# 512-column bfloat16 products on TensorE, and an earlier masked product on VectorE, in two attention-like stages of a two-block network

## The reference, cut to what matters

```python
def one_block(args):                      # differential attention, 8 heads, blocks of 128 queries
    qblk, start = args
    s = jnp.einsum('bqhcd,bkhcd->bhcqk', qblk, k).astype(jnp.float32) * scale
    s = jnp.where(mask, s, -jnp.inf)
    p = jax.nn.softmax(s, axis=-1)
    attn = p[:, :, 0] - lam * p[:, :, 1]
    return jnp.einsum('bhqk,bkhe->bqhe', attn.astype(v.dtype), v)
...
# state-space mixer: 16 heads in 4 groups
cb = jnp.einsum("bclgn,bcsgn->bcgls", cm, bm)
y_diag = jnp.einsum("bcgls,bgecls,bcsgep->bclgep", cb, decay_in, x_dt)
states = jnp.einsum("bclgn,bgecl,bclgep->bcgepn", bm, decay_states, x_dt)
y_off = jnp.einsum("bclgn,bcgepn,bgecl->bclgep", cm, prev, jnp.exp(a_cum))
```

## Time and profile before

| | us |
|---|---|
| three runs shown | 3040.71, 3015.47, 3042.67; median 3040.71 |
| profiled execution, its own time | 3019.05 |
| its span | 3017.3 |
| TensorE busy in it | 2626.9 (87%) |
| VectorE busy | 1455.2 (48%) |
| ScalarE busy | 957.2 (32%) |
| mean granted clock of TensorE | 0.865 |

### The profile page before, as it was taken

One profiled execution on the slowest core, in us unless ns is written; L12 is line 12 of the kernel. 1 busy time (PEld: TensorE's weight loads), 2 busy tenths in 40 slices (PEclk: granted clock), 3 DMA queues, 4 the chain that ended last, 5 costly groups with the idle time before them and its releaser, 6 DMA issues.

```text
span 3017.3 us, 39461 instructions
## 1 busy us (share of the span) xinstructions
PE 2626.9 (87%) x16258; PEld 1729.5 (57%) x16258; DVE 1455.2 (48%) x2253; ACT 957.2 (32%) x1535; POOL 73.4 (2%) x60
## 2 busy tenths in 40 slices
PE   6979999999989886899998997757785989899997
PEld 5768878888878653544445445544443456444443
DVE  4773435552255355365324453454445343477742
ACT  3321223322232443332222332114443234343321
POOL 0610000000000000000000000000000000000000
PEclk9975578999979876799998995658897999999998
DMA  3100001232312200022321310000001133023221
GB/s 140 71 1 29 29 29 56 85 112 84 112 39 83 84 1 1 28 87 109 112 84 56 112 72 28 1 15 1 30 1 56 56 112 112 29 84 112 76 95 67
DMA packets 27731, 188.08 MB, mean 62 GB/s; under 512 B 3072, under 2 KB 3584, under 8 KB 6048
## 3 DMA queue, kind: packets, MB, share of 16 engines
q1 hardware_dynamic: 27072, 183.77, 16.6%
q10 hardware_dynamic: 480, 1.79, 0.2%
HBM read 183.45 MB, written 2.10 MB: 61 GB/s over the span
## 4 chain that ended last, share of the span: by engine, by line
PE 78%; DVE 13%; ACT 6%; issue 2%; DMA 1%; DVEq 0%; ACTq 0%; POOL 0%; SPq 0%; POOLq 0%
PE ps L428 37%; PE ps L425 20%; PE ps L538 3%; PE ps L1044 1%; DVE wsp L409 1%; ACT wsp L398 1%; PE ps L586 1%; PE ps L1390 1%; DVE wk L2486 1%; PE ps L1032 1%; PE ps L881 1%; PE ps L1412 1%; DMA raw_w<-slabs 1%; PE ps L556 1%; PE ps L948 1%
## 5 line engine op out<-in xcount | busy, mean ns | idle before, releaser
L428 PE MATMUL ps<-hn,wsp 128*128 128x512 f16 x3120 | 689.6, 385 | 28.9 <-DVEq L226 10.3
L428 PEld LDWEIGHTS ps<-hn,wsp 128*128 128x128 f16 x3120 | 308.2, 99 | 409.4 <-issue 30.4
L409 DVE SCALAR_TENSOR_TENSOR wsp<-raw_w,wsp 128x2048 f16<-128x2048 f32 (+1 forms) x176 | 389.7, 2214 | 316.3 <-ACT wsp L398 305.8
L428 PE MATMUL ps<-big,wsp 128*128 128x512 f16 (+2 forms) x2304 | 465.8, 364 | 5.0 <-DVE wk L2111 2.8
L425 PE MATMUL ps<-hn,wsp 128*128 128x264 f16 x3552 | 413.6, 280 | 13.3 <-DVE hn L378 7.8
L425 PEld LDWEIGHTS ps<-hn,wsp 128*128 128x128 f16 x3552 | 351.8, 99 | 74.1 <-issue 14.6
L398 ACT ACTIVATE wsp<-raw_w 128x2048 f16<-128x2048 f32 (+1 forms) x176 | 324.7, 1845 | 167.5 <-PE ps L425 66.4
L428 PEld LDWEIGHTS ps<-big,wsp 128*128 128x128 f16 (+1 forms) x2304 | 230.6, 100 | 233.8 <-issue 6.1
L425 PE MATMUL ps<-big,wsp 128*128 128x264 f16 x1920 | 218.9, 277 | 0.1
L425 PEld LDWEIGHTS ps<-big,wsp 128*128 128x128 f16 x1920 | 188.3, 98 | 30.0 <-ACT hn L415 0.3
L415 ACT ACTIVATE wk<-ps 128x512 f32<-128x512 f32 (+2 forms) x116 | 69.0, 595 | 346.9 <-PE ps L428 345.6
(11 more groups left out here) (353 smaller groups left out, 2744.6 us busy)
## 6 DMA issues: line engine op xcount, KB each, us to landing
raw_w<-slabs SPq DMA_DIRECT2D x166, 1024.0 KB, 5.2
raw_w<-slabs SPq DMA_DIRECT2D x8, 384.0 KB, 5.0
h<-xin SPq DMA_DIRECT2D x1, 2112.0 KB, 8.6
out<-hn SPq DMA_DIRECT2D x8, 256.0 KB, 2.8
big<-memx ACTq DMA_DIRECT2D x1, 1024.0 KB, 5.3
cst<-consts SPq DMA_DIRECT2D x1, 995.5 KB, 9.7
sml<-small SPq DMA_DIRECT2D x1, 768.0 KB, 12.1
wk<-ropes ACTq DMA_DIRECT2D x1, 528.0 KB, 3.7
```

What stands on the lines that cost most here:

```text
L409: L.fin(L.eng.scalar_tensor_tensor(wsp[:, n % NW, 1, lo:hi], raw_w[:, q % 2, 0:hi - lo], WSCALE, wsp[:, n % NW, 0, lo:hi], ALU.mult, ALU.s ...
L428: return L.eng.matmul(ps[:rows, b, 0:T], lhsT, rhs, start=start, stop=stop)
```

## The change

There are three edits. A new helper, `keep_warm(L, b, k)`, issues k matmuls on TensorE, each with the 128x128 bfloat16 identity `eye16` as weights and the first 512 bfloat16 values of the constant `ssd_mask` as the moving operand, into PSUM bank b. Nothing reads the result, and a later matmul with `start=True` overwrites the bank. It has four of them in each of the 16 units of the state-space part, between the wait for `mx` and the wait for `ysum`, and four in the 31 turns of the attention's loop that have a next unit, between its values and the transposes of the next one. And on VectorE the masked product of group g+1 now comes ahead of the sums of group g, and that of group 0 right after the chunk's `xw`.

```diff
+        def keep_warm(L, b, k):
+
+            for _ in range(k):
+                L.eng.matmul(ps[:, b, :], eye16, C("ssd_mask").bitcast(BF16)[:, 0:512], start=True, stop=True)
...
                     pe.wait_ge(sem("mx"), n + 1)
+                    keep_warm(L, r, 4)
                     pe.wait_ge(sem("ysum"), n) if n else None
...
                 l1_values(n)
                 if n + 1 < 32:
+                    keep_warm(L, 6, 4)
                     l1_turn_pe(n + 1)
...
+            def mixed(n):
+
+                L.take("dm")
+                L.fin(tt(Mx[:, n % 2, :, :], Dm[:, n % 2, :, :],
+                         ps[:, 2 + n % 2, 0:P].unsqueeze(1).to_broadcast([P, 4, P]), ALU.mult), "mx")
+
             for c in range(SSD_NC):
...
                 L.fin(tt(xw, xdt, dlast[:, c, :].unsqueeze(2).to_broadcast([P, 16, 64]), ALU.mult), "xw")
+                mixed(4 * c)
                 for g in range(4):
                     n = 4 * c + g
-                    L.take("dm")
-                    L.fin(tt(Mx[:, n % 2, :, :], Dm[:, n % 2, :, :],
-                             ps[:, 2 + n % 2, 0:P].unsqueeze(1).to_broadcast([P, 4, P]), ALU.mult), "mx")
+                    if g < 3:
+                        mixed(n + 1)
                     L.take("py")
```

## The result

Changed kernel: median 3007.8 us of 13 runs (2988.5 to 3010.4). Kernel before: median 3038.5 of 13 runs (3015.5 to 3044.2). The ratio is 0.9908, 95% interval 0.9887 to 0.9929: 28 us faster, or 22 to 34 by the interval (the two medians alone lie 30.7 us apart). The forecast on the median was 16 us less and a time of 3025; the time lies in the range given, but the gain is nearly twice the forecast one. At 0.9% by the ratio (0.7 to 1.1% by its interval) it stands at the very line of 1% at which the chances were divided, and it is clear of noise.

The account below looks back on a forecast made before the run. TensorE, busy 87% of the span, was taken to bound the kernel, with both stages partly at the low clock. Attention −9 and state-space −7 gave −16 us, from a median of 3041 to 3025 us, range 2994 to 3046.

Parts of the forecast that it names:

- What a group costs: Four added products on TensorE cost 0.85 us at the high clock or 1.7 us at the low one.
- the 18 us of the bound: Both stages: if weight loads lay between the products, 0.4 us more per group, 18 us for 47 groups.
- Attention, the clock and the place of the groups: Attention loop: clock stays high, groups of queries 0 and 1 hide in the output-copy wait; −9 us.
- The short units: Attention, queries 2 and 3: TensorE's work summed to 4.05 us each, against 4.50 and 4.71.
- The starting point: Profiled execution of 3019 us as base, less 16; median of 3041 lies 22 us above it, unexplained by the trace.
- State-space part: Clock gains of −5, −2 and −2, group costs of +4.5, VectorE's order −3: together −7 us.
- −5 for chunk 0: State-space chunk 0: three units at the high clock save 7.5 us; one unit lost before the clock rises leaves −5.
- a clock over 0.85 until the chunk's end: State-space part: granted clock expected if the forecast was right.
- The wait of about 1.1 us at group 3: State-space group 3: TensorE's expected wait for line 2050 behind the added group, if the forecast was right.
- VectorE's order: State-space part: masked product leaves the path, 0.73 us off group 3's wait, −3 us over 4 chunks.
- The rule about busy work: Skill's rule that sustained busy work releases the throttle; if true, the sum would be some 8 us worse in chunk 0.
- more than forecast: Rival: short attention units fall to 3.6 (16 us), all four chunks run high (12 us): −28, 3013; chance 0.10.

Follow-up runs that it names:

- e3: Kernel before with only VectorE's new order and no added products: 3031.7 us, ratio 1.0009 to the kernel before.
- e7: Changed kernel with four more products ahead of each of the 16 steps of the first block's recurrent mixer: 2969.5 us, ratio 0.9781 to the kernel before.
- e8: Changed kernel with the attention's products only in the turns of queries 0 and 1: attention 132.5 us, ratio 0.9848 to the kernel before.
- e9: Kernel before with four products per state-space unit, in bank 4 and ahead of the wait for `mx`, VectorE's old order: state-space part 111.6 us.
- e13: Changed kernel with the state-space products moved to bank 4 and ahead of the wait for `mx`, VectorE's new order: state-space part 115.0 us.
- e14: Changed kernel plus products in the recurrent mixer and at chunk ends, state-space products ahead of the wait, new order: 2962.2 us, ratio 0.9745 to the kernel before.
- e15: Changed kernel plus products in the recurrent mixer and at chunk ends, state-space products ahead of the wait, but old order: 2964.9 us, ratio 0.9751 to the kernel before.
- e4: Changed kernel with added products of 16 rows instead of 128, same 512 columns: 3075.1 us, ratio 1.0165 to the kernel before.

## Why the prediction was right or wrong

**What a group costs: right.** 0.87 us at the high clock (0.85), loads hidden: with 188 products in two stages the 18 us of the bound did not appear.

**Attention, the clock and the place of the groups: right.** The clock is 0.96 (0.95 or more was asked), the steps 4.18 and 4.78 (4.19 and 4.77), the whole 132.3 us (about 132). The whole agrees in part by luck. The short units are shorter than summed, 3.78 and 3.77 instead of 4.05: the sum divided the duration of a group by its count, but in the rows each starts before the one ahead of it has ended: after the six values the next group starts 0.87 us on (1061.98 to 1062.85), not 1.0, and after the four transposes 0.44 us on (1064.14 to 1064.58), not 0.7. A few steps with a fall of the clock make up for it, which the sum did not have; the changed kernel's second profile has 134.8.

**The starting point: this is the step that failed.** Between the two profiles the stages shrank by 14.7 us, near the 16 forecast. What failed is that the kernel before was taken to be as its one profile shows it, and that the 22 us between this profile and the median was carried over unchanged. For the attention the prediction took "141.9 / 31 = 4.58 us for a unit, 18.3 for a head" as what the kernel before does. At the low clock throughout, a head takes 20.4 us (5.12 + 5.91 + 4.02 + 5.33 between the output copies in e3, whose stretch is the row below), at the high clock and with the groups 16.5, and what a run gets is a mixture that changes from execution to execution.

```profile
1076.10:1096.50 20.40, 18.86 (x70) 11.87 (x70) 10.44 (x33) 8.86 (x29) 0.00 (x0) 0.50 0.00 1
```

The profile had the best of six. Against their mean of 147.3, and a mean of 133 for the profiles with the full groups (132.3, 134.8, 132.5, 134.6, 132.5), the gain is 14 us, where the sum had 9.

**State-space part: right in sign, and mis-sized in the same way.** The gain against the profile used was 5.1 (7 forecast). Chunk 0 gained 3.9 us in the one profile of the changed kernel and 6.6 in the other, chunks 1 and 2 2.7 and 1.6, and chunk 3 lost 3.1. The sum had −5 for chunk 0, but left out the 1.7 us of the group in the unit that it took as lost; with it, its own terms give −3.4. It also gave chunk 1 "one short drop to 0.50", where its clock was 0.71 over 36.5 us, and it counted 17 us at the low clock in chunk 0, where 38.1 us ran at 0.55. The sign "a clock over 0.85 until the chunk's end" did not come: the four chunks had 0.72, 0.85, 0.77 and 0.88. The wait of about 1.1 us at group 3 did come. Against the unchanged profiles' mean of 128.1, the changed ones' mean (119.8 and 116.9; e7 115.2 and e8 119.8 have the same code there) of 117.9 is 10 us less. 14 + 10 = 24 us lies in the measured 22 to 34, near its lower end. What an execution near 3041 does in these stages no profile caught; the profiled executions of before ended at 3019, 3024 and 3034. And how often the recurrent mixer's short run comes in the one kernel and the other is open. Of the changed kernel's 13 times two lie near 2990 and the others at 3004 to 3010, a distance like the mixer's 16 us. Their clocks fit it: 0.889 and 0.888, against 0.880 to 0.884, make by my estimate (twice the span times 1 − clock) 663 and 670 us at the low clock, against 696 to 722, and the mixer's two lengths differ by 44 us of it. That is a likeness and no proof.

**VectorE's order: the wait was sized right, the term was wrong.** "−3 us" was counted for it, 0.73 a chunk. Where the clock is the same in both orders, some 0.6 us a chunk is there (the wait of group 3 in e9 and e13, chunk 0 of e14 and e15). But alone it gives nothing in the time (e3), and beside products ahead of the wait the whole part was 3 us longer with it in both pairs (115.0 against 111.6, 111.7 against 108.7), in a chunk at a lower clock; the times don't tell the two orders apart. It did have a use that I named only as a place, not as a condition: with the products behind the wait for `mx`, as the change has them, the old order makes the part 143.3 us. The order lets that place be harmless; the better place makes the order needless.

**The rule about busy work: the trace was right to overrule it.** The reading that a busy TensorE gets the high clock (the Trainium skill, TensorE: Matmul & The Clock Gate, Part 1) does not agree with e4, where 96% busy went with 0.57, if busy is what the profile calls busy.

**The chances.** 0.25 for faster by over 1% stands beside a ratio of 0.9908, and 0.67 for within 1%: neither is refuted by a gain of 0.9%. The 28 us are those of the rival "more than forecast", but neither of its conditions came: the short units stayed at 3.78 us and not 3.6, and chunks 0 and 2 did not run high. The text said that no likely case reaches 30 us "from its mechanism alone", and that followed from the one profile. Two of the three times shown lay 22 us above it, which the prediction noted and then left as an offset common to both kernels. It was no plain offset: in the three profiles of before the two stages together take 266.7, 273.7 and 277.9 us (sums of the table), and the executions took 3019, 3024 and 3034. So 11 of the 15 us between the first and the third lie in the very stages that the change shortens.

## What to carry to other kernels

A stage of small products with a mean granted clock between the two levels doesn't have one length. Before summing against it, price it at both levels and take the spread of the runs as a sign of where it usually is; a change that holds the level gains that spread too. Spare products pay where they stand ahead of a wait that TensorE has anyway, into a bank that is free by then; one line later, behind the wait of a loop that VectorE closes, the same products made the part 32 us longer (143.3 against 111.6). And look first at the longest stretch that is busy at the low clock: here it was one that the change left alone, and it was worth more than both of the others: 35 us in its own stretch, 38 in the median.

## What the runs showed of the hardware

- Granted clock and busy share can go opposite ways: 96% busy at 0.57 with 16-row products (e4), 85% busy (113.28 of 132.55 us) at 0.96 with 128-row ones.
- A 512-column bfloat16 product with 16 rows takes as long as one with 128: four in 1.02 and 1.04 us.
- The same instructions took 153.3 to 169.9 us in the recurrent mixer in different executions, at 0.67 and 0.57.
- Products whose result nothing reads can shorten a stage: 134.1 us at 0.90 instead of 169.7 at 0.57 in the recurrent mixer, with 16 groups of four more in it (e7).
